# Triangular inverses of a chunked delta rule on Trainium2: both directions multiplied together on the four quarters of the array, and the weight parts between them dealt out anew

## What is computed

```python
a_mat = jnp.where(strict, jnp.einsum('bhncd,bhnsd->bhncs', kb, k) * decay, 0.0)
sol = lax.linalg.triangular_solve(eye + a_mat, rhs, left_side=True, lower=True, unit_diagonal=True)
...
o_f, s_f = _gated_delta_rule(q, k, v, g[0], beta[0], s0_f)
o_b, s_b = _gated_delta_rule(jnp.flip(q, 2), jnp.flip(k, 2), jnp.flip(v, 2),
                             jnp.flip(g[1], -1), jnp.flip(beta[1], -1), s0_b)
```

## Time and profile before

| | |
|---|---|
| median of 3 runs | 2294.05 us (2288.71 to 2294.27) |
| the profiled execution | 2285.42 us, span 2283.6 us |
| TensorE matmul busy, whole span | 2212.3 us (97%) |
| VectorE, ScalarE, GpSimd busy | 870.6, 793.4, 1013.7 us |
| granted TensorE clock, mean | 0.998 |
| recurrence, 272 to 530 us: TensorE, VectorE, ScalarE, GpSimd busy | 238.17, 158.83, 102.77, 86.01 us |

### The profile page before, as it was taken

How to read it: one execution, slowest core, us unless ns; L and a number is a source line. 1 busy time by engine, 2 the same in 40 slices (tenths; PEclk the granted TensorE clock), 3 DMA queues, 4 the chain that set the end, 5 groups by cost and what they waited for, 6 DMA issues and landing times.

```text
span 2283.6 us, 37010 instructions
## 1 busy us (share of the span) xinstructions
PE 2212.3 (97%) x14690; PEld 1790.0 (78%) x14690; DVE 870.6 (38%) x1533; ACT 793.4 (35%) x1256; POOL 1013.7 (44%) x469
## 2 busy tenths in 40 slices
PE   6999999989999999999999999999999999899999
PEld 5789867777678888878878888887888887658999
DVE  4566566565511311353471131133122113665212
ACT  3445444433432132232233223224222221554453
POOL 0357622343344444434434444443444444205888
PEclk9999999999999999999999999999999999999999
DMA  8335476455443333325324333322423333203666
GB/s 283 93 105 159 136 259 223 148 187 206 155 153 124 93 93 96 97 102 184 92 93 157 113 99 92 92 92 83 166 93 94 93 99 92 71 19 112 186 190 186
DMA packets 90931, 297.56 MB, mean 130 GB/s; under 512 B 8992, under 2 KB 21664, under 8 KB 90400
## 3 DMA queue, kind: packets, MB, share of 16 engines
q1 hardware_dynamic: 90640, 295.05, 40.1%
q10 hardware_dynamic: 144, 0.34, 0.1%
HBM read 294.31 MB, written 1.05 MB: 129 GB/s over the span
## 4 chain that ended last, share of the span: by engine, by line
issue 55%; POOL 23%; PE 16%; DVE 2%; DMA 1%; ACT 1%; POOLq 1%; SPq 1%; DVEq 0%; ACTq 0%
POOL w_lo L571 23%; PE bank L599 3%; PE bank L603 3%; PE bank L600 3%; PE bank L643 2%; PE bank L1614 1%; PE bank L1625 1%; DVE gdn_outer L1984 1%; PE bank L1593 1%; PE bank L1067 1%; PE bank L1530 1%; DMA first_mods<-in_modstream 0%; DVE gdn_outer L1986 0%; PE bank L1637 0%; POOLq L576 0%
## 5 line engine op out<-in xcount | busy, mean ns | idle before, releaser
L571 POOL TENSOR_TENSOR w_lo<-w_raw,w_hi 128x1024 fp32r<-128x1024 f32 x379 | 923.1, 2439 | 1091.0 <-ACT w_hi L839 1090.6
L599 PE MATMUL bank<-n_hi,w_lo 128*128 128x512 f32 (+1 forms) x2216 | 789.0, 356 | 12.7 <-POOL w_lo L571 5.7
L603 PE MATMUL bank<-n_lo,w_hi 128*128 128x512 f32 (+1 forms) x2216 | 782.5, 353 | 2.5 <-DVE n_lo L757 2.1
L600 PE MATMUL bank<-n_hi,w_hi 128*128 128x512 f32 (+1 forms) x2216 | 781.6, 353 | 0.0
L839 ACT CAST w_hi<-w_raw 128x1024 fp32r<-128x1024 f32 x383 | 402.6, 1053 | 764.2 <-PE bank L603 740.3
L599 PEld LDWEIGHTS bank<-n_hi,w_lo 128*128 128x128 f32 x2216 | 416.4, 188 | 91.4 <-issue 16.6
L603 PEld LDWEIGHTS bank<-n_lo,w_hi 128*128 128x128 f32 x2216 | 416.4, 188 | 69.7 <-DVE n_lo L757 4.1
L600 PEld LDWEIGHTS bank<-n_hi,w_hi 128*128 128x128 f32 x2216 | 416.7, 188 | 63.2
L2390 DVE TENSOR_TENSOR prod<-silu,bank 128x512 f32<-128x512 f32 (+1 forms) x88 | 54.5, 620 | 717.8 <-PE bank L603 710.6
L599 PE MATMUL bank<-g_hi,w_lo 128*128 128x512 f32 (+1 forms) x768 | 283.2, 369 | 1.7 <-DVE g_lo L2381 1.7
L603 PE MATMUL bank<-g_lo,w_hi 128*128 128x512 f32 (+1 forms) x768 | 282.9, 368 | 0.0
(11 more groups left out here) (386 smaller groups left out, 1878.7 us busy)
## 6 DMA issues: line engine op xcount, KB each, us to landing
w_raw<-in_stream SPq DMA_DIRECT2D x383, 512.0 KB, 3.6
late<-in_modstream SPq DMA_DIRECT2D x56, 512.0 KB, 4.6
mod_raw<-in_modstream SPq DMA_DIRECT2D x48, 512.0 KB, 5.9
w_raw<-in_modstream SPq DMA_DIRECT2D x48, 512.0 KB, 6.0
first_mods<-in_modstream SPq DMA_DIRECT2D x6, 1024.0 KB, 10.8
h<-in_tokens SPq DMA_DIRECT2D x2, 1024.0 KB, 6.2
first_mods<-in_modstream SPq DMA_DIRECT2D x4, 512.0 KB, 9.1
consts<-in_consts SPq DMA_DIRECT2D x1, 1152.0 KB, 5.9
```

What stands on the lines that cost most here:

```text
L571: nc.gpsimd.tensor_tensor(w_lo[:, slot, :], w_raw[:, slot, :], w_hi[:, slot, :].bitcast(F32), ALU.subtract).then_inc(w_lo_ready, 1)
L599: nc.tensor.matmul(out_ap, wl, hi, start=start, stop=False)
L600: nc.tensor.matmul(out_ap, wh, hi, start=False, stop=False)
L603: return nc.tensor.matmul(out_ap, wh, lo, start=False, stop=stop)
```

## The change

Levels 2 to 4 of both directions are issued together, head by head: two products of F, two of B. B is put on the other two quarters. For that its `left` writes each half's product into the other half of PSUM, and its `right` reads the swapped halves; the transposed inverse `xc` of B must lie swapped as well, so that after levels 1 to 3 VectorE transposes it in two instructions of 64 partitions, not in one of 128. `left_both` waits for both directions' sums, `right_both` for both copies and both transpositions. The slots are dealt anew: two parts after level 2's left ("left2") and two after its right ("right2"), and two fewer in "half" and in "key"; ScalarE's copies and VectorE's bias sums for them follow.

```diff
-    MOD_SLOTS = {"first": 2, "half": 4, "last": 2, "key": 4}
+    MOD_SLOTS = {"first": 2, "left2": 2, "right2": 2, "half": 2, "last": 2, "key": 2}
...
+        def crossed(d, i):
+            return half(1 - i) if d == BWD else half(i)
+
+        def left_both(r, li):
+            batches = per_batch(r)
+            for n, d, t, hs, b0, gc in batches:
+                if li == 2:
+                    pe.wait_ge(p_lev, nth(2, r, 0, d))
+                elif li == 3:
+                    pe.wait_ge(p_lev, nth(2, r, 1, d))
+                pe.wait_ge(d_xm, nth(5, r, li - 1, d))
+            for j in range(4):
+                for n, d, t, hs, b0, gc in batches:
+                    w = W[d]
+                    a_li = w["a2"] if li == 2 else w["al"][:, li - 3]
+                    for i in range(2):
+                        last = nc.tensor.matmul(upper(b0 + 1, crossed(d, i))[:, j], a_li[half(i), j],
+                                                w["xtc"][half(i), j], start=True, stop=True)
+                    if j == 3:
+                        last.then_inc(g_p1, 1)
+
+        def right_both(r, li):
+            batches = per_batch(r)
+            for n, d, t, hs, b0, gc in batches:
+                pe.wait_ge(a_t1, nth(6, r, li - 1, d))
+                pe.wait_ge(d_xt, nth(5, r, li - 1, d))
+            for j in range(4):
+                for n, d, t, hs, b0, gc in batches:
+                    w = W[d]
+                    for i in range(2):
+                        last = nc.tensor.matmul(packed(b0 + 1, half(i))[:, j], w["xc"][crossed(d, i), j],
+                                                w["t1h"][crossed(d, i), j], start=True, stop=True)
+                    if j == 3:
+                        last.then_inc(g_p2, 1)
...
-            for d in (FWD, BWD):
-                left(r, 2, d)
-            for d in (FWD, BWD):
-                right(r, 2, d)
-            for d in (FWD, BWD):
-                left(r, 3, d)
+            left_both(r, 2)
+            some_mods(r, "left2")
+            right_both(r, 2)
+            some_mods(r, "right2")
+            left_both(r, 3)
             if step_ == 2:
...
-            for d in (FWD, BWD):
-                right(r, 3, d)
-            for d in (FWD, BWD):
-                left(r, 4, d)
+            right_both(r, 3)
+            left_both(r, 4)
             for d in (FWD, BWD):
                 keys_state(r, d)
-            for d in (FWD, BWD):
-                right(r, 4, d)
+            right_both(r, 4)
...
             for d in (FWD, BWD):
                 tail_copy(r, 2, d)
+            mods_copied(r, "left2")
+            mods_copied(r, "right2")
...
-            nc.vector.transpose(flat(w["xc"]), flat(w["xtc"])).then_inc(d_xt, 1)
+            if d == BWD and li < 4:
+                for i in range(2):
+                    last = nc.vector.transpose(flat(w["xc"])[half(1 - i)], flat(w["xtc"])[half(i)])
+            else:
+                last = nc.vector.transpose(flat(w["xc"]), flat(w["xtc"]))
+            last.then_inc(d_xt, 1)
...
+            turned_groups(r, "left2")
             for d in (FWD, BWD):
                 add_level(r, 2, d)
+            turned_groups(r, "right2")
```

## The result

| | before | changed |
|---|---|---|
| median | 2291.38 us | 2314.47 us |
| ratio, 95% interval | | 1.0112 [1.0088, 1.0135] |
| once more, on another chip (median) | 2285.15 us | 2310.80 us |
| ratio, 95% interval | | 1.0111 [1.0097, 1.0126] |
| profiled execution, span | 2285.42, 2283.6 us | 2311.04, 2309.2 us |

A forecast was written before the change was run, and what follows sets the result against it. It took a ring of engines without slack in the recurrence as the bound. 9.2 + 10.0 - 5.3 - 3.4 + 0.5 = +11.0 us: 2296.4 for a profile, 2305 for the median, range 2298 to 2315 (8 in 10).

The forecast's parts named there:

- ring: Rounds 1 to 7, level 2's left to level 4's right: joined levels lengthen the chain of engines, +10.0 us in all.
- key: End of a round: two fewer parts give back up to 0.85 us where the next left follows straight; -3.4 us in all.
- Clock: Round 0: TensorE idle some 6 us, so part of it runs at 1.2 GHz; +0.5 us (0 to 2).
- E: Rival on the recurrence's clock: passes and `keys_state` lengthen by up to 0.5 and 2 us, 3 to 11 in all; chance 0.06.
- Round 0: Moved parts wait for loads in level 2, so line 1719 comes at 300.4 against 291.20: +9.2 us, bounds 8.5 to 11.
- The level: One joined level takes 3.73 us against 2.5: left to right 1.72, right to the next left 2.01.
- The slots of level 2: Rounds 1 to 7: two slots of 1.0 us hide under the joined level's waits and cost nothing; uncovered, 2 us a round.
- Rounds 4 and 5: Queries by keys between left and right hide the copies: levels +0.2 us each, and +0.35 in round 4 for the turn.
- Round 3: Levels 2 to 4 grow by 1.8 us, as a state sum already slowed level 2 before.
- B: Rival: parts stop round 0 less long, or the level is 3.4 us; +2 to +6.5 us, 2296 to 2300; chance 0.14.
- C: Rival: TensorE's issue paces a level, so joining leaves it at or under 2.5 us; 2280 us, chance 0.05.
- D: Rival counted among the cases slower by over 0.3%; its claim, size and chance are missing from the text given.

The follow-up runs named there:

- the filled kernel: Changed kernel plus useless 128x512 products in the gaps of levels 3 and 4 and at round 0's wait: 2304.95 us, 1.0086; again 2305.82 us, 1.0088.
- the fuller one: Changed kernel with round 0's old slots, useless products in the gaps and one more behind right of level 4 in every round: 2296.27 us, 1.0035.

## Why the prediction was wrong in size

Round by round, in us against the kernel before. "Forecast" adds up the prediction's terms for a round (ring, half, last, key). "At full clock" is the length of the round in a kernel with the changed structure and no half clock in it (0 to 5 from the filled kernel's rows above; 6 and 7 from the two runs with round 0 as before, filled 33.89 and unfilled 22.02 us), less that before. "Half clock" is the time at 1.2 GHz that the window rows of the changed kernel give.

| round | forecast | at full clock | measured | half clock |
|---|---|---|---|---|
| 0 | +8.9 | +8.2 | +12.4 | 20.6 |
| 1 | +1.15 | +1.1 | +4.7 | 10.0 |
| 2 | +1.4 | +1.6 | +3.1 | 3.2 |
| 3 | +1.6 | +2.3 | +4.4 | 7.1 |
| 4 | -1.1 | -0.2 | +1.3 | 3.1 |
| 5 | -2.5 | -1.6 | -1.6 | 0 |
| 6 | +0.55 | +0.8 | +2.2 | 3.5 |
| 7 | +0.5 | +0.6 | +2.2 | 3.3 |
| sum | +10.5 | +12.9 | +28.7 | 51 |

**The step that failed is "Clock".** It put 0.5 us, bounds 0 to 2, and looked only at the 6 us in which TensorE waits for the loads. The rounds show 28.73 - 12.87 = 15.9 us, of which 0.8 is a stall in round 1: 0.2 to 0.5 us of time for each us at half clock, in every round that has some and in none that hasn't. (The second profile of the changed kernel, without a stall, gives 15.1, or 15.9 with the 36.3 us that round 0 takes in the second one of the filled kernel.) The filling bears it out on one chip: 10.3 us less within the rounds and 5.4 kept in the two where the clock still falls. The other terms together came out at +12.9 instead of +10.5. The sign that was misread stood in the sum itself: the join turns F's and B's passes of 0.68 us, laid in each other's gaps, into one of 0.69 and bare gaps of 0.94 and 1.38 us. As a cost for the ring that was counted, and as a lighter load for TensorE it was a rival, E. Its mechanism is the right one, passes and `keys_state` that lengthen by up to 0.5 and 2 us: the pass went from 0.69 to 1.13, `keys_state` from 2.05 to 3.55. It was held to "some 1 to 2 us in a few rounds", 3 to 11 in all, and to 0.06, on the ground that the kernel before has a clock of 1.00. But that row describes the load before the change, not the load that the change makes.

**Round 0** was right in its mechanism and nearly in size, with some luck. Line 1719's successor (line 1750) starts at 302.11 after, at half clock; in the filled kernels, at full clock, it starts at 300.37 and 300.47, against 300.4. But their rounds start 0.7 and 1.6 us later than before, so that this is 8.5 and 7.7 us and not 9.2. The wait of line 643 is 6.49 us against 7. Its load was issued at 283.40, 1.0 us later than counted, and landed in 3.6 us instead of the 4.3 that I took for the least (over the whole recurrence of before the least is 3.4). That left of level 3 comes at 291.49 against 291.6 is luck: no second stand, and half clock in its place.

**The level** was right: 1.63 + 2.07 = 3.70 us against 3.73; the two copies in a row take 0.65 where 0.84 was counted, and the two sums with their transpositions a little more.

**The slots of level 2** are hidden, as forecast: left to right and right to left are 1.63 and 2.07 us with the parts between them. In round 4, with the turn in it, left to right takes 2.21.

**Rounds 4 and 5** are each 0.9 worse than forecast. With sixteen 128x128 instructions between left and right I counted 2.44 us and it is 2.61, and in round 5 it is 3.14 in level 4: the second half of keys by the state waits for VectorE's state update. The keys slot gave back 0.6 instead of 0.85 in round 4. **Round 3** has 0.3 more in the ring than forecast and 0.4 behind level 4.

**Rivals.** B fell (the wait is there). C fell: the level is 3.7 us, far from the 2.9 at which TensorE's issue would pace it. D fell by the 0.69 us pass, and by the run on two quarters. E, with a chance of 0.06, named what happened and held it too small. The Trainium skill, page "TensorE: Matmul & The Clock Gate", Part 1, gives a floor of about 25 ns from one start to the next; 32 starts within 0.69 - 0.22 = 0.47 us are 15 ns apart, so the measurement decides against it here.

**What stays open.** The rounds say 15 to 16 us for the clock; of the whole time the first filling gets 5.0 back, and the fuller one, with round 0 as before, 7 to 9. The difference is partly half clock that the filling leaves (round 6 of the first filled kernel has 6.8 us of it and a stall of 1.4, and lasts 37.74 us where 33.9 are possible) and partly the stretch behind the recurrence, which took 1759.0 to 1766.4 us in the profiles of all kernels. Why the clock also falls in some filled rounds without a stall, and why it fell so much in rounds 0 and 1 on two quarters, where TensorE had more to do, I can't say.

## What to carry over

Joining two interleaved chains into one wide step saves the engine's time and opens its gaps: count it only where other work of the same engine covers the copies and sums between the steps, as in rounds 4 and 5 here, where join and new slots pay 2.2 us a round (0.9 of it by the join with the slots of the change, the rest by moving "first" too). A granted clock of 1.00 in the profile of before says nothing about the clock after a change that takes work out of a dense stretch; cost the change at both levels of the clock. And before parts are moved ahead in an engine's order, look at the landing time of the first that depends on a load: the slots moved in round 0 cost some 9 us, a third of the whole loss, 6 to 7 of it without the clock.

## What the runs showed of the hardware that was not expected

- Half clock outlasts the gaps in front of it: in round 0 it held from 294.5 to 308.2, the last 9 us of it with TensorE busy throughout (8.85 us of matrix work in 299 to 308).
- At 1.2 GHz the small products lengthen less than the large ones: a joint pass of 32 from 0.69 to 1.13 us (1.6 times), a part's four 128x512 instructions from 1.05 to 1.92 (1.8 times).
- Useless work can make a kernel faster: 2310.80 to 2305.82 us on one chip, and 1.0075 to 1.0035 in another pair, by filling alone.
- TensorE can stop for 0.5 to 1.7 us inside a pass of independent instructions with no wait that the profile shows, at another place from kernel to kernel; 1.41 us in round 6 of the first filled one.
